# Bringing an expert's output back: low parts of the second slot block folded in by VectorE, three placing products a piece in place of four

## The reference, cut to what matters

```python
def swiglu(x, w1, w3, w2):
    return (jax.nn.silu(x @ w1) * (x @ w3)) @ w2

def moe_swiglu(x, w_router, b_router, w1, w3, w2):
    xt = x.reshape(-1, d)
    logits = (xt @ w_router).astype(jnp.float32) + b_router.astype(jnp.float32)
    top_v, top_i = lax.top_k(logits, TOP_K)                  # TOP_K = 2
    gates = jax.nn.softmax(top_v, axis=-1)
    dense_gate = jnp.sum(jax.nn.one_hot(top_i, N_EXPERTS, dtype=jnp.float32) * gates[..., None], axis=1)
    y = jnp.zeros_like(xt)
    for e in range(N_EXPERTS):                               # N_EXPERTS = 8
        y = y + dense_gate[:, e:e + 1].astype(x.dtype) * swiglu(xt, w1[e], w3[e], w2[e])
    return y.reshape(bsz, seq, d)
```

## Time and profile before

| | us |
|---|---|
| median of 3 runs | 3275.53 |
| lowest and highest | 3273.42, 3278.61 |
| the profiled execution, its time | 3277.59 |
| the profiled execution, span of its trace | 3275.8 |
| experts, from the first gathering to the last piece added | about 1455 to 2229 of the span |

### The profile page before, as it was taken

How to read it: one execution, slowest core, us unless ns; L and a number is a source line. 1 busy time by engine, 2 the same in 40 slices (tenths; PEclk the granted TensorE clock), 3 DMA queues, 4 the chain that set the end, 5 groups by cost and what they waited for, 6 DMA issues and landing times. The chain is left out here.

```text
span 3275.8 us, 45166 instructions
## 1 busy us (share of the span) xinstructions
PE 2839.7 (87%) x17726; PEld 2369.7 (72%) x17726; DVE 1705.8 (52%) x2738; ACT 1039.7 (32%) x1477; POOL 518.0 (16%) x396
## 2 busy tenths in 40 slices
PE   7987686999978647869999999996999997999996
PEld 6887674877767636868998888895675585766495
DVE  5736554323243863356666665665455446456445
ACT  3341122222111103124454444542243342233342
POOL 0114311313200610012221222220000000000000
PEclk9998887999989878959999999998999997999998
DMA  3220002223228421116655555553221112221021
GB/s 128 85 78 3 2 1 90 90 84 98 75 91 209 136 53 43 53 54 198 211 171 168 179 172 168 198 173 100 66 64 41 53 52 68 78 69 51 17 78 52
DMA packets 269147, 311.29 MB, mean 95 GB/s; under 512 B 22848, under 2 KB 242496, under 8 KB 268096
## 3 DMA queue, kind: packets, MB, share of 16 engines
q1 hardware_dynamic: 257616, 301.29, 28.7%
q10 hardware_dynamic: 11376, 7.87, 1.0%
HBM read 302.31 MB, written 4.19 MB: 94 GB/s over the span
## 5 line engine op out<-in xcount | busy, mean ns | idle before, releaser
L2151 PE MATMUL ps<-moe_xy,moe_w_hi 128*128 128x384 f32 x1408 | 406.4, 362 | 3.0 <-DVE moe_xy L2243 3.0
L1944 DVE TENSOR_TENSOR moe_w_lo<-ring,moe_w_hi 128x2048 fp32r<-128x2048 f32 x144 | 312.6, 2171 | 109.9 <-ACT moe_w_hi L1939 109.7
L2154 PE MATMUL ps<-moe_xy,moe_w_lo 128*128 128x192 f32 x1408 | 354.6, 252 | 0.0
L1939 ACT ACTIVATE moe_w_hi<-ring 128x2048 fp32r<-128x2048 f32 x144 | 254.8, 1769 | 63.2 <-PE ps L256 57.7
L2154 PEld LDWEIGHTS ps<-moe_xy,moe_w_lo 128*128 128x128 f32 x1408 | 269.2, 191 | 0.0
L2151 PEld LDWEIGHTS ps<-moe_xy,moe_w_hi 128*128 128x128 f32 x1408 | 265.3, 188 | 4.1 <-issue 4.1
L259 PE MATMUL ps<-ring_r,x_feat_r 128*128 128x256 f32 (+2 forms) x576 | 187.4, 325 | 0.0
L256 PE MATMUL ps<-x_feat_r,ffn_w_hi 128*128 128x512 f32 x352 | 140.3, 399 | 16.3 <-DVE ffn_w_lo L1944 16.3
L2717 ACT ACTIVATE s_sb<-s_sb,att_small 128x128 f32<-128x128 f32 (+3 forms) x128 | 71.8, 561 | 258.9 <-DVE att_small L2709 257.8
L260 PE MATMUL ps<-x_free_r,ring_r 128*128 128x512 f32 x368 | 148.3, 403 | 0.0
L2287 POOL TENSOR_TENSOR moe_hid_hi<-moe_prod,cst 128x384 fp32r<-128x384 f32 (+1 forms) x48 | 60.4, 1258 | 550.8 <-DVE moe_prod L2258 550.8
(11 more groups left out here) (562 smaller groups left out, 7388.7 us busy)
## 6 DMA issues: line engine op xcount, KB each, us to landing
ring<-in_moe_w SPq DMA_DIRECT2D x120, 1024.0 KB, 5.2
ring<-in_w_in SPq DMA_DIRECT2D x32, 1024.0 KB, 5.3
ring<-in_ffn_w SPq DMA_DIRECT2D x30, 1024.0 KB, 5.3
ring<-in_w_ada SPq DMA_DIRECT2D x24, 1024.0 KB, 5.8
ring<-in_gdn_w_in SPq DMA_DIRECT2D x12, 1024.0 KB, 5.8
ring<-in_moe_w SPq DMA_DIRECT2D x24, 512.0 KB, 3.8
ring<-in_s_w_glu SPq DMA_DIRECT2D x8, 1024.0 KB, 5.3
ring<-in_w_out SPq DMA_DIRECT2D x8, 1024.0 KB, 5.0
```

The costliest lines, as they stand in the source:

```text
L1939: self.prog.nc.scalar.activation(self.flat(self.hi, j % SPLITS, j), self.raw(j), ACT.Copy).then_inc(self.hi_done, 1)
L1944: self.prog.nc.vector.tensor_tensor(self.flat(self.lo, j % SPLITS, j), self.raw(j), self.flat(self.hi, j % SPLITS, j).bitcast(F32), ALU.su ...
L2151: mm = nc.tensor.matmul(out, wh[:, k, cs], both[:, k, :], start=(k == 0), stop=False)
L2154: mm = nc.tensor.matmul(out[:, 0:SLOTS], wl[:, k, cs], xg[0][:, k, :], start=False, stop=(k == KD - 1))
```

## The change

The low part of the second slot block is no longer kept as an operand of its own. ScalarE writes the high part of rows 0 to 63 only. VectorE subtracts it from the PSUM rows 0 to 63 and writes the difference to rows 64 to 127 of a scratch tile (`rest`, in slot 3 of `ring`), waits for itself, and adds rows 64 to 127 of the PSUM bank to it, into rows 64 to 127 of `y[0]`. So `y[0]` holds in its second block the high parts above and all the rest below, and one product with `put` sums them. The second block's product with `y[1]` is gone: a piece takes three products.

```diff
+    rest = prog.weights.ring[:, RAW, 0:2 * BANK].rearrange("p (b n) -> p b n", n=BANK)
...
-                for n, (s, part) in enumerate((s, part) for s in range(2) for part in range(2)):
-                    mm = nc.tensor.matmul(ps[:, 4 + i % 4, :], put[:, s, t], y[part][:, s, cs], start=(n == 0), stop=(n == 3))
+                for n, (s, part) in enumerate(((0, 0), (0, 1), (1, 0))):
+                    mm = nc.tensor.matmul(ps[:, 4 + i % 4, :], put[:, s, t], y[part][:, s, cs], start=(n == 0), stop=(n == 2))
...
-                nc.scalar.activation(y[0][:, i // 2, (i % 2) * BANK:(i % 2 + 1) * BANK], ps[:, 4 + i, :], ACT.Copy
+                rows = slice(0, P) if i < 2 else slice(0, SLOTS - P)
+                nc.scalar.activation(y[0][rows, i // 2, (i % 2) * BANK:(i % 2 + 1) * BANK], ps[rows, 4 + i, :], ACT.Copy
...
-                nc.vector.tensor_tensor(y[1][:, i // 2, cs], ps[:, 4 + i, :], y[0][:, i // 2, cs].bitcast(F32),
-                                        ALU.subtract).then_inc(y_lo, 1)
+                if i < 2:
+                    nc.vector.tensor_tensor(y[1][:, i // 2, cs], ps[:, 4 + i, :], y[0][:, i // 2, cs].bitcast(F32),
+                                            ALU.subtract).then_inc(y_lo, 1)
+                else:
+                    upper, lower = slice(0, SLOTS - P), slice(SLOTS - P, P)
+                    nc.vector.tensor_tensor(rest[lower, i % 2, :], ps[upper, 4 + i, :], y[0][upper, 1, cs].bitcast(F32),
+                                            ALU.subtract).then_inc(y_rest, 1)
+                    dve.wait_ge(y_rest, e * 2 + (i - 1))
+                    nc.vector.tensor_tensor(y[0][lower, 1, cs], ps[lower, 4 + i, :], rest[lower, i % 2, :], ALU.add
+                                            ).then_inc(y_lo, 1)
```

More of the change, by code:

```diff
@@ L2084, in sparse_parts @@
              "silu_done", "mult_done", "hi_ready", "hid_ready", "down_ready", "y_hi", "y_lo", "back_ready", "back_done",
-             "cross_copied", "halves_added")
+             "cross_copied", "halves_added", "y_rest")
     (prepared, pick_ready, gathered, g_hi, g_lo, put_ready, put_act, put_dve, up_ready, silu_done, mult_done,
-     hi_ready, hid_ready, down_ready, y_hi, y_lo, back_ready, back_done, cross_copied, halves_added) = (st.counter(n) for n in names)
+     hi_ready, hid_ready, down_ready, y_hi, y_lo, back_ready, back_done, cross_copied, halves_added, y_rest) = (st.counter(n) for n in names)
     acc_ready = st.counter("acc_ready")
```

## The result

| | us |
|---|---|
| before, median of 6 runs beside it | 3277.61 (3273.42 to 3279.22) |
| changed, median of 6 runs | 3287.78 (3287.36 to 3291.82) |
| ratio, 95% interval | 1.0036 (1.0023 to 1.0049) |
| profiled execution of the changed kernel, and its span | 3287.36, 3285.5 |

What follows compares the result with a forecast made beforehand. TensorE bounds the kernel, busy 87%, with a stop set by VectorE at each expert's end. First sum -2.2 and clock +11.7 give +9.5 on 3277.59, 3287.1; set against the runs' median, 3285.0 us; range 3273 to 3293.

Steps and rivals of the forecast that it cites:

- The products: TensorE's placing at an expert's end: eight products fewer at 0.230 us each, -1.84 us an expert.
- VectorE's chain: Low parts ahead of placing: two more VectorE instructions lengthen TensorE's stop by 1.5 us (+1.44 to +1.6), to about 3.3.
- VectorE as the bound of the placing: Additions behind placing: 0.751 us each against 0.69 a piece on TensorE, so VectorE becomes the bound; ends +0.23 us.
- the bound of the copy: Copy after an expert's additions: VectorE's idle 0.60 us absorbs its delay, so the copy moves with TensorE, -0.34 us.
- The first sum, without the clock: Experts' ends: seven passages give -2.4 us, the last expert's additions +0.2, together -2.2 us (-2.9 to +1.5).
- The clock: Placing behind the longer stops: seven falls to 1.2 GHz at 1.9 us, less one of 1.64 already there, +11.7 us.
- The comparison with other stops of 2.7 to 3.9 us: Six such stops elsewhere in the trace: clock at or near 0.50 behind five, so seven of eight ends fall.
- Rival 1: Experts' ends: the clock holds, falls at three ends at most; 3273.3 us with one fall, 3278 with three; chance 0.35.
- Rival 2: VectorE's moves between row halves cost twice 0.69 us, stop 4.7 us, clock falls every time; 3296 us, chance 0.04.
- Rival 3: Experts' placing: branch not taken, or VectorE's extra work hidden and 14.7 us gained, 3260.8 us; chance 0.03.

Runs made afterwards that it cites:

- e4: Kernel before with three products a piece and nothing else changed, the second slot block's low part left out of the sum; 3261.1 us, ratio 0.9953.
- e6: Changed kernel with the second block's subtractions and additions all on rows 0 to 63, its low parts not placed; 3276.3 us, ratio 1.0004.
- e8: Changed kernel with eight of its 24 needed placing products issued early, in TensorE's stop; 3278.9 us, ratio 1.0011.
- e1: Changed kernel with 15 unneeded filling products on TensorE in each expert's stop; 3276.2 us, ratio 0.9999.
- e2: Kernel before with 8 unneeded filling products on TensorE in each expert's stop; 3275.3 us, ratio 1.0000.
- e11: Second trace of e6, with nothing else changed; 3274.7 us, one run.
- e10: Changed kernel with four unneeded filling products in each expert's stop; 3282.7 us, ratio 1.0020.
- e3: Kernel before with VectorE's two subtractions and their waits added, four products a piece kept, results unused; 3298.7 us, ratio 1.0072.
- e12: Second trace of the changed kernel, with nothing else changed; 3288.7 us, one run.

## Why the prediction was right, point by point

- **Direction and size.** Forecast 3285.0, measured 3287.8, in the range and slower by more than 0.2% as forecast. The median of before was 3277.6 in its six runs, so the forecast difference was 9.5 us and the measured one 10.2. That these agree to 0.7 us is luck in part: by the terms below, as the traces have them, the sum is about +12 (13.1 - 0.9), and the interval of the ratio reaches from +7.5 to +16.
- **The products:** -1.84 us an expert, measured 1.83 to 1.84 (7.53 less 5.70), and 14.8 us in all when taken away alone (e4).
- **VectorE's chain:** predicted +1.5 (+1.44 to +1.6), measured +1.69, outside the bounds. The term that was too small is what an instruction costs that can't overlap the one ahead: I took 0.08, the difference to a mean of 0.635, but that mean mixes a first step of 0.70 (1.39 less 0.69 above) with later ones of 0.60. The price is 0.12 twice, and e6 shows it. Taking +1.5, near the end without the late starts, was too low as well: they came about, twice a chain, with a longer delay than the 0.08 I had put on them. The stop came out at 3.46, not 3.3.
- **VectorE as the bound of the placing:** wrong. I took 0.75 us for an addition in a row and 0.70 as the lower bound. Additions follow one another in 0.68 us in e4, where they keep up with pieces of 0.69, and in 0.66 in e8, where they wait for nothing ((5.36 - 0.75) / 7). The lower bound came from the same mean of 0.635. In e4, where the clock holds, VectorE has 0.51 us of idle time left before the copy. It cost the sum nothing, since TensorE was put down as the bound of the copy anyway.
- **The first sum, without the clock:** predicted -2.2 us (-2.9 to +1.5); e1 against e2 gives -0.13 us an interval, -0.9 over seven, and medians that can't be told apart. For seven intervals the prediction had -2.4: too favourable by 1.5 us, 1.3 of it the chain's 0.19 an expert.
- **The clock:** predicted 7 falls at 1.9, less one of 1.64, +11.7; measured eight, 1.34 to 1.66 us at six ends and 2.74 and 2.92 at two (each placing less 5.70), 14.7 us in all, less 1.64: +13.1. So 1.84 a fall on average, near the 1.9 taken. This error of 1.4 us and that of the last point go the same way and add up. The comparison with other stops of 2.7 to 3.9 us led to about the right count, but that was luck in part: in e6, with 0.25 us less of a stop and 95.6 us between stops, it is two, and the stop of e6, 3.21 us, is nearer to the forecast's 3.3 than the 3.46 of the changed kernel.
- **Rival 1**, by which the clock holds, did not come about here, yet it is what e6 does at six ends of eight. (Its time with three falls should read 3276.6 by its own terms, 3273.3 and 3.3, not 3278.) The Trainium skill's warning, page "TensorE: Matmul & The Clock Gate", section "HAM oscillation — how this bites in real kernels", is of long idle gaps only; measured here, gaps of 1.84, 2.55 and 3.23 us cost the clock too, at one, four and eight ends of eight, and the measurement decides. **Rival 2** (dear moves between the halves) is out by the durations: 0.685 and 0.695 us. **Rival 3** is out by 64 products fewer in the page and a stop of 3.46 us.

## What to carry to other kernels

An instruction moved from the busy engine to an idle one is not free where the busy engine waits for the idle one: here 1.83 us of products were bought with 1.69 us of a stop, and the low clock behind the stop then cost 1.84 us more. Before such a trade, look at the clock behind every stop of TensorE that it lengthens, and count what a fall costs in the next products. Where a stop can't be shortened, put needed products into it: the same eight products in the stop brought 14 us with no arithmetic saved.

## What the runs showed of the hardware that was not expected

- A longer stop of TensorE need not lower the clock more often: 3.21 us did at two ends of eight (e6, e11), 2.55 us at four (e10), and one stop of 3.45 us did not (e3).
- A VectorE instruction that starts at another row of the tile than the one ahead begins 0.72 us behind it and not 0.60 (64 rows of 512 elements); its duration is 0.01 us longer.
- The ends at which the clock falls were the same in a second trace, for two kernels: e6 and e11 at the first two ends only, the changed kernel and e12 at all eight, with the same two long ones (8.44 and 8.40 us, 8.62 and 8.56 us). Stops of 3.21 and 3.23 us differed between two and eight falls with 0.2 us more between them; why is open.
